# A hybrid decoder trunk on one core: where five short serial stretches stand, and what is moved around them

## The reference, cut to what matters

```
Layer i (i even: native sparse attention, i odd: gated DeltaNet):
  h = RMSNorm(x); proj = h @ W_in[i] -> [token-mixer columns | memory-query columns]
  token mixer (causal) in parallel with 4-head cross-attention into 256 memory tokens
  x = x + concat(mixer_out, memory_out) @ W_out[i]
  x = x + relu(RMSNorm(x) @ W_up[i])**2 @ W_down[i]
y = RMSNorm(x)
```

## Time and profile before

| | us |
|---|---|
| median of 3 runs | 1996.64 (1996.47 to 1998.94) |
| the profiled execution | 2001.48 |
| its span, first to last instruction | 1999.7 |
| PE busy in it | 1893.6 (95%) |
| DVE busy | 1049.5 |
| ACT busy | 520.3 |

### The profile page before, as it was taken

The page is one execution under the profiler, slowest core; times in us unless marked ns, Lnnn a source line. Parts: engine busy times, 40 slices in busy tenths (PEclk is TensorE's granted clock), DMA queues, the critical chain, the costliest instruction groups (busy, mean ns, idle before and its releaser), DMA issues.

```text
span 1999.7 us, 26775 instructions
## 1 busy us (share of the span) xinstructions
PE 1893.6 (95%) x10027; PEld 1522.5 (76%) x10027; DVE 1049.5 (52%) x2334; ACT 520.3 (26%) x1294; POOL 39.5 (2%) x48
## 2 busy tenths in 40 slices
PE   7999999998979999999989999899998999999997
PEld 6788555666758888888877787688876888888885
DVE  4441777655565444454446665456555544444444
ACT  2221777233312212100012523333341212210000
POOL 0000000000001000000010000000000000000001
PEclk9999999999989999999999999999998999999998
DMA  6532200566422222222233112100012122222211
GB/s 229 190 129 64 80 1 1 169 195 184 149 106 84 85 85 84 73 78 83 85 121 136 64 64 68 74 1 1 32 41 72 66 85 85 84 85 85 85 64 45
DMA packets 60801, 175.46 MB, mean 88 GB/s; under 512 B 6529, under 2 KB 39442, under 8 KB 47362
## 3 DMA queue, kind: packets, MB, share of 16 engines
q1 hardware_dynamic: 58050, 163.05, 24.4%
q0 software_dynamic: 2624, 10.70, 1.3%
HBM read 160.80 MB, written 12.93 MB: 87 GB/s over the span
## 4 chain that ended last, share of the span: by engine, by line
PE 82%; DVE 6%; SPq 5%; ACT 4%; issue 3%; DMA 1%; POOL 0%; DVEq 0%; POOLq 0%; ACTq 0%
PE psum L1818 58%; PE psum L1341 5%; SPq L492 3%; PE psum L758 2%; PE psum L902 2%; SPq L487 1%; PE psum L739 1%; ACT sbuf L802 1%; PE psum L721 1%; DVE sbuf L1677 1%; PE psum L1796 1%; PE psum L641 1%; PE psum L1899 1%; PE psum L1893 1%; PE psum L1931 1%
## 5 line engine op out<-in xcount | busy, mean ns | idle before, releaser
L1818 PE MATMUL psum<-sbuf 128*128 128x272 f32 x5152 | 1196.1, 393 | 4.5 <-ACT sbuf L2093 1.4
L1818 PEld LDWEIGHTS psum<-sbuf 128*128 128x128 f32 x5152 | 972.7, 190 | 215.6 <-issue 11.3
L1341 PE MATMUL psum<-sbuf 128*128 128x128 f32 (+3 forms) x1020 | 125.8, 279 | 12.4 <-DVE sbuf L1661 5.2
L1341 PEld LDWEIGHTS psum<-sbuf 128*128 128x128 f32 (+3 forms) x1020 | 118.7, 191 | 19.5 <-DVE sbuf L1661 6.0
L2043 ACT ACTIVATE sbuf<-sbuf 128x544 f32<-128x544 f32 x32 | 20.8, 651 | 396.9 <-DVE sbuf L2387 387.5
L902 PE MATMUL psum<-sbuf 128*128 128x256 f32 x448 | 106.7, 389 | 7.1 <-DMA sbuf<-in_pages 7.1
L2266 DVE TENSOR_TENSOR sbuf<-sbuf 128x512 f32<-128x512 f32 x92 | 63.4, 689 | 81.4 <-PE psum L1818 73.6
L902 PEld LDWEIGHTS psum<-sbuf 128*128 128x128 f32 x448 | 82.8, 190 | 24.0 <-DMA sbuf<-in_pages 8.1
L2270 DVE TENSOR_TENSOR sbuf<-sbuf 128x512 f32<-128x512 f32 x92 | 63.8, 693 | 52.2 <-PE psum L1818 50.5
L1520 ACT ACTIVATE sbuf<-psum 128x384 f32<-128x384 f32 (+2 forms) x84 | 40.2, 480 | 106.0 <-PE psum L1341 80.8
L2279 DVE TENSOR_TENSOR sbuf<-sbuf 128x512 f32<-128x512 f32 x92 | 63.1, 686 | 0.0
(11 more groups left out here) (390 smaller groups left out, 2026.9 us busy)
## 6 DMA issues: line engine op xcount, KB each, us to landing
sbuf<-in_w SPq DMA_DIRECT2D x100, 1024.0 KB, 4.9
sbuf<-in_pages SPq DMA_DIRECT2D x256, 128.0 KB, 2.4
sbuf<-in_mcache SPq DMA_DIRECT2D x2, 4096.0 KB, 15.4
sbuf<-in_win SPq DMA_DIRECT2D x8, 512.0 KB, 4.8
out_win_o<-sbuf POOLq DMA_DIRECT2D x8, 512.0 KB, 3.0
sbuf<-in_state SPq DMA_DIRECT2D x6, 512.0 KB, 5.7
out_state_s<-sbuf POOLq DMA_DIRECT2D x6, 512.0 KB, 3.1
sbuf<-in_x SPq DMA_DIRECT2D x1, 2176.0 KB, 11.9
```

Source lines behind the costliest of these rows:

```text
L1341: last = mm(bank(pair[x])[0:rows, width * (h - h0):width * (h - h0 + 1)], lhs(h), rhs(h), start=True, stop=True)
L1818: ins = mm(to, lhs(k), rhs(k), start=first and k == 0, stop=k == 3, skip_group_check=True)
```

## The change

1. **Begin.** SP issues panel 1 before x. PE does three products into an unused bank as soon as the constants are there (`idle_work`), then sums each of the memory tokens' squares as it comes. The squares of x are added on DVE into `rstd` (seven additions, `first_squares`, behind the 16 `memn`), and PE makes only two products for them (`first_norm_sums`), which stand between the memory keys and values of layer 0 and those of layer 1. The first half of layer 0's keys waits for `memn` tile by tile.
2. **Norms 2 and 4.** PE sums the squares with the tokens as output partitions: ten matmuls of one column, five from `sq_sum` and five from the last tile (`token_norm_sums`). DVE adds the two (128x5), ACT takes the root and DVE the reciprocal of 128x5, and PE spreads the result over the partitions with six matmuls against the identity, into banks 6 and 7. `norm` reads it there. `single` of the second input layer therefore goes into banks 4 and 5.
3. **Entry of the recurrence.** The gates of chunk 0 are made in unit 11 of the input layer, with the two memsets, the running sums on PE behind the first product of unit 12 (in banks 4 and 5), the exponents on DVE in unit 12, the exponentials and the root on ACT between its last two reads of unit 12. Behind the last product PE starts at once with k·k and q·k of chunk 0, and waits for the last read only after them. The SiLU of the last gates is waited for in the last chunk.
4. **Exit of the recurrence.** The reciprocal of the samples' lengths and the weight sums stand ahead of the last state addition on DVE; `spread_samples` stands behind the first product of the output layer, and its scaling on DVE behind the memory part of the input sums (`after_last`).

```diff
@@ begin
             panel(0)
+            panel(1)
             sp.dma_start(xT, x_in).then_inc(in_x, 16)
-            for i in range(1, 4):
-                panel(i)
+            panel(2)
+            panel(3)
...
             def memory_sums():
                 pe.wait_ge(in_common, 16)
-                pe.wait_ge(mem_sq, KT)
+                idle_work(pe, 5, 3)
                 for k in range(KT):
+                    pe.wait_ge(mem_sq, k + 1)
                     last = mm(bank(0)[:, 0:MEM], ones, sqm[:, k, :], start=k == 0, stop=k == KT - 1)
...
             memory_sums()
-            for k in range(KT):
-                square_sums(k)
-            memory_kv()
+            memory_kv(0)
+            first_norm_sums()
+            memory_kv(1)
...
+            def first_squares():
+                for k in range(1, KT):
+                    dve.wait_ge(sq_ready, k + 1)
+                    if k > 1:
+                        dve.wait_ge(dve_step, k - 1)
+                    tt(rstd, rstd, sq[:, k % 2, :], ALU.add).then_inc(dve_step, 1)
@@ norms 2 and 4
+            def token_norm_sums(n):
+                pe.wait_ge(sq_added, 6 * n)
+                for ci, at in enumerate(BLOCKS):
+                    mm(bank(6)[:, ci:ci + 1], sq_sum[:, at:at + P], ones[:, 0:1], start=True, stop=True)
+                pe.wait_ge(sq_ready, (n + 1) * KT)
+                for ci, at in enumerate(BLOCKS):
+                    last = mm(bank(7)[:, ci:ci + 1], sq[:, 1, at:at + P], ones[:, 0:1], start=True, stop=True)
+                last.then_inc(sq_used, 1)
+                pe.wait_ge(dve_step, RSTD_READY[n])
+                for ci, lo, hi in SPREADS:
+                    half, at = lo // HALF, BLOCKS[ci]
+                    last = mm(both(3)[:, half, lo - HALF * half:hi - HALF * half],
+                              rstd_t[:, ci:ci + 1].to_broadcast([P, P]), ident[:, lo - at:hi - at], start=True, stop=True)
+                last.then_inc(pe_step, 1)
@@ entry
+                    if (g, place) == (GDN_U - 1, 1):
+                        running_sums(pe, 0)
...
+                if not ci:
+                    pe.wait_ge(*read_out(ubase["gdn_in"] + GDN_U - 1, "c11"))
+                    pe.wait_ge(dexp_ready, 1)
...
+                    if t == 2 * GDN_U - 2:
+                        decays(act, 0)
+                        act.wait_ge(ks_read, 1)
+                        f(kr, kr2, ACT.Sqrt).then_inc(kr_ready, 1)
...
+                    if g == 11:
+                        decay_rows(dve, 0)
+                        dve.memset(st_p, 0.0)
+                        dve.memset(wq, 0.0)
+                    if g == 12:
+                        exponents(dve, 0)
@@ exit
+            def samples_between(g, place):
+                if (g, place) == (0, 1):
+                    spread_samples(pe)
+                if (g, place) == (0, 2):
+                    pe.wait_ge(cn_ready, GH + 1)
...
+                        dve.wait_ge(cn_std, 2)
+                        dve.reciprocal(rinv[0:TS, 4, :], rinv[0:TS, 4, :]).then_inc(cn_rec, 1)
+                        before_last()
                     dve.wait_ge(sdec_ready, h + 1)
                     dve.wait_ge(snew_mm, h + 1)
                     tt(sg[h], sg[h], view(banks(6, 2), 2, 4, P), ALU.add).then_inc(snew_ready, 1)
-            before_last()
-            dve.wait_ge(cn_std, 2)
-            dve.reciprocal(rinv[0:TS, 4, :], rinv[0:TS, 4, :]).then_inc(cn_rec, 1)
+            after_last()
             dve.wait_ge(cn_bc, GH + 1)
```

More of the change, by code:

```diff
@@ L615, in build, with idle_work @@
         scored = lambda g: 8 * (g // 2) + 1 + max(m for m in range(8) if PAIR[m][0] == g % 2)
+        def idle_work(pe, b, n):
+            for _ in range(n):
+                pe.matmul(bank(b)[:, 0:256], ident, common_ap[:, 0:256], start=True, stop=True)
         def compress_prompt(pe):
@@ L1328, in spread_samples, with decay_rows, running_sums, exponents @@
             last.then_inc(cn_bc, 1)
+        sums_in = lambda ci: BD if ci else (4, 5)
+        def decay_rows(dve, ci):
+            R, U = CHUNKS[ci][0], GC["cum" if ci < 4 else "cum_s"]
+            dve.tensor_tensor(ug[0:R, :, 0:R], U[0:R, 0:R].unsqueeze(1).to_broadcast([R, GH, R]),
+                              bcast(gat[0:R, ci, :], R, GH, R), ALU.mult).then_inc(ug_ready, 1)
+        def running_sums(pe, ci):
+            R = CHUNKS[ci][0]
+            pe.wait_ge(ug_ready, ci + 1)
+            pe.wait_ge(nwt_ready, 2 * ci)
+            for x, (h0, h1) in enumerate(HALVES):
+                last = pe.matmul(bank(sums_in(ci)[x])[:, 0:R * (h1 - h0)], ones[0:R, :], ug[0:R, h0:h1, 0:R],
+                                 start=True, stop=True)
+            last.then_inc(gc_done, 1)
+        def exponents(dve, ci):
+            R, MASK = CHUNKS[ci][0], GC["mask" if ci < 4 else "mask_s"]
+            dve.wait_ge(gc_done, ci + 1)
+            for x, (h0, h1) in enumerate(HALVES):
+                for h in range(h0, h1):
+                    last = dve.scalar_tensor_tensor(
+                        out=dec[0:R, h, 0:R], in0=bank(sums_in(ci)[x])[0:R, R * (h - h0):R * (h - h0 + 1)],
+                        scalar=gcn[0:R, ci, h:h + 1], in1=MASK[0:R, 0:R], op0=ALU.subtract, op1=ALU.subtract)
+            last.then_inc(gc_ready, 1)
+        def decays(act, ci):
+            R = CHUNKS[ci][0]
+            act.wait_ge(gc_ready, ci + 1)
+            act.activation(dec[0:R, :, 0:R], dec[0:R, :, 0:R], ACT.Exp, scale=-1.0)
+            for x, (h0, h1) in enumerate(HALVES):
+                last = act.activation(egr[:, h0:h1, 0:R], view(bank(sums_in(ci)[x])[:, 0:R * (h1 - h0)], h1 - h0, R),
+                                      ACT.Exp)
+            last.then_inc(dexp_ready, 1)
         def pe_gdn(pe):
@@ new lines, in memory_kv @@
+            def memory_kv(l):
+                pe.wait_ge(in_panel[2 * l], 16)
+                wk, wv = view(ring[2 * l], KT, MEM), view(ring[2 * l + 1], KT, MEM)
+                for hp in range(2):
+                    for k in range(KT):
+                        if hp == 0:
+                            pe.wait_ge(memn_ready, KT * l + k + 1)
+                        last = mm(bank(1 + 2 * l)[:, MEM * hp:MEM * (hp + 1)], wk[:, k, P * hp:P * (hp + 1)],
+                                  memn[:, l, k, :], start=k == 0, stop=k == KT - 1)
+                last.then_inc(pe_out, 1)
+                pe.wait_ge(in_panel[2 * l + 1], 16)
+                for m in range(2):
+                    for k in range(KT):
+                        last = mm(bank(2 + 2 * l)[:, MEM * m:MEM * (m + 1)], memn[:, l, k, P * m:P * (m + 1)],
+                                  wv[:, k, :], start=k == 0, stop=k == KT - 1)
+                last.then_inc(pe_out, 1)
```

161 lines of the change are left out of this document (65 added, 96 removed).

## The result

The changed kernel takes 1984.90 us, the median of five executions from 1978.18 to 1985.44, against 1996.64, which is a median of five too. The ratio is 0.9933 with a 95% interval from 0.9922 to 0.9943: faster by 0.7%, where 1.3% was forecast, and 5 us above the range's upper end. The profiled execution took 1984.69 (span 1982.9). Against the 2001.48 of the profiled execution before, that is 16.8 us, where the sum promised 26.8; between the medians it is 11.7.

The account below looks back on a forecast made before the run. PE, busy for 95% of the span, was taken as the bound. Gains of 9.1 + 3.2 + 1.3 + 8.7 + 4.5 = 26.8 us off the median of 1996.64 gave 1970, range 1966 to 1980.

Parts of the forecast that it names:

- the sum: Whole kernel: gains at begin, norm 2, norm 4, entry and exit add up to 26.8 us.
- The clock eats a part: PE's new gaps and the exit leave it at 1.2 GHz: gain 19.2 us, time 1977, chance 0.20.
- the fall of the clock in the idle 2.8 us: Begin, ahead of layer 0's keys: the clock might fall while PE idles, costing another 1.7 us.
- PE's idle spell falls apart into two of about 1 us, so the clock should stay up: Norm 2: the product behind was to take 7.37 us and not 9.13, another 1.8 of the 3.2 us gain.
- the size of the spreading: Norm 2: 12 records on PE at 0.145 us each, 1.75 us in all.
- the bound that was given: Norm 4: gain of 0.3 us with spreading at the lower clock, where 1.3 was forecast.
- the decays don't hide: Entry, unit 12: ACT's exponentials come late and PE waits ahead of k·k; gain 21.1 us, time 1975.5, chance 0.09.
- slower: Recurrence: the clock falls before its first chunk and stays down, +57 us at full length; chance 0.04.
- I take 4.5, a clock that rises between: Exit: gain of 4.5 us, taken between 2.2 at the lower level and 6.3 at best.
- the upper bound of 6.3: Exit: the first output product brings the clock up at about 1512, DVE becomes the limit, gain 6.3 us at best.
- the 0.5 us that the prediction estimated: Norm 4: reading the scale from PSUM makes the eight scalings 0.5 us longer; not added to the sum.

Follow-up runs that it names:

- the kernel with all fills: Changed kernel plus idle products ahead of layer 0's keys, and wide sums with two idle products in norms 2 and 4 and at the exit: 1969.36 us, ratio 0.9856.

## Why the prediction came out as it did

**The direction was right, and the mechanism was one of its rivals.** "The clock eats a part" gave 19.2 us and a chance of 0.20. The trace gave 16.8, and each of its places is the one that the rival named; the time of 1977 it missed too, for a reason given below. And the kernel with all fills, which adds to PE's work and differs in the clock, gives 1969.4. That the parts are worth less is out: with all fills the kernel is 1998.18 - 1969.36 = 28.8 us ahead of the one before, more than the 26.8 of the sum; the exit alone then gives 6.8 and not 4.5. A reading of the prediction was off as well: PE's second longest wait, 7.9 us at L974 for DVE's L1176, is missing from its list of the largest; the change leaves it as it is.

**Begin.** The step that failed is the value taken between its bounds: the fall of the clock in the idle 2.8 us stood there as a bound (1.7) and was left out of the sum. It happened (1.9) in all seven profiles that have this gap behind the change's own idle products: the keys took 8.85 us in six and 8.74 in one. It did not come in the gap, but 1.3 us into the keys, and in the kernel without the change's idle products the same gap went without it (7.17). The memory's sums ended 0.5 late, inside their range. Removing x's squares, the additions that hide behind the keys and the scalings that end before `single` all went as worked out.

**Norm 2.** The step that failed reads "PE's idle spell falls apart into two of about 1 us, so the clock should stay up". It argued from the length of the gap alone and took no account of the work ahead of it: behind the one-column records the clock fell in all seven profiles, in one of them with the gap of 1.00 us filled; behind 96-column records of nearly the same duration, in front of the same gap, it stayed up, in the one profile that has the width without a filling and in two that have both. With that fell the size of the spreading (1.75 forecast, 2.77 measured; 1.52 where the clock stayed up) and of the product. The -1.1 of the table is not the price of the change: it sets 17.50 against an execution whose old norm 2, at 16.38, was the quickest of three. On average the gain is 0.6. That the rival had 0.6 too is chance: by the terms beside it, 1.4 less the 1.25 that a spreading of 3 and not 1.75 costs and nothing from the product, it should have read 0.2.

**Norm 4** is the same step, with 0.3 at the lower level, the bound that was given.

**Entry.** Right in place and in size: 8.7 forecast, 9.0 between the traces, 8.6 by the kernel with the old entry, and 9.7 between the medians. The rival "the decays don't hide" is out: ACT was free at 1265.0 and waited 1.69 us for PE at its last read, where 1.6 were forecast. So is "slower": from 1267 to 1445 us, over the chunks of the prompt, the granted clock was 1.00. (Where the samples' chunk begins it was 0.83 for 20 us, in both kernels.) The table load that was moved costs what the earlier trace rows showed, 1.28 us, and the trace has the next operation 1.30 us behind its start. The Trainium skill (ScalarE: Activation LUTs, What ACT_TABLE_LOAD costs) gives 1283 ns for the load, with which the trace agrees, and a drain of 1380 ns besides, which this trace doesn't show; an estimate from that figure, 2.8 us for ACT's two loads in unit 12, would have eaten the 1.6 us that were left.

**Exit.** The step that failed is "I take 4.5, a clock that rises between". Its lower end was 2.2 for a clock that stays low until the end, and 1.9 was measured. The prediction read the lower level as coming "after idling", of 4.00 us, and let the first product, put directly behind the state products, bring the clock up at about 1512. But the kernel before was at that level ahead of those 4.00 us: its granted clock was 0.95 in the window at 1504 us and 0.50 at 1505, and its last state products already took 3.77 us, against 1.98 in the heads before. Its timeline, 1491 to 1545 us:

```profile
1505.12 0.80 PE L1311 MATMUL psum<-sbuf 128*32 128x1 f32 x12 [0.82 <-ACT sbuf L1501]
1505.85 3.77 PE L1468 MATMUL psum<-sbuf 32*128 32x512 f32 x4
```

The changed kernel keeps this piece as it is, and the clock falls there again, at 1490 us. It was back 17 us later in both profiles, with the 4.00 us idle or busy, and 7 us later in the three of the changed exit that took 18.0. So closing the gap did not by itself bring the clock back sooner. Over seven profiles the changed exit lies at 21.54, 18.0 (three times), 21.53, 21.55 and 20.05, on average 19.8, against 22.7 for the two of the kernel before: 2.9. With the fill it is 15.9, 6.8 less, a little above the upper bound of 6.3, and then DVE's reads are the limit (waits of 0.41, 1.05 and 0.62 us in PE's timeline), as that bound had it.

**The sum's base.** The profiled execution before, 2001.48, lay 4.8 above its median, and two of the stretches with a price here differ by 1.4 us between its executions. A further 3.3 us between two executions of the kernel before lie in the 989 us from `single` to norm 2, which the change doesn't touch; what makes them I haven't found. This is also why the medians are further off than the traces: 11.7 and not 26.8 is 15.1 short, 10.0 by the parts and 5.1 because the profiled execution before was slow for its kernel and the one after was not. Measured again, the changed kernel was 19.5 ahead (1998.18 - 1978.69), inside the prediction's range and close to the rival's 19.2. Which of the two medians one gets is luck, so the number says less about the rival than its four places do.

**PSUM as a source.** The eight scalings took 5.62 us with the scale in PSUM, against 5.66 from SBUF. The sum added nothing for it and was right; the 0.5 us that the prediction estimated from the Trainium skill (VectorE: DVE Perf Modes, TRN2 errata) are not there.

**Open.** What decides whether the clock falls in a single execution: the same instructions gave norm 2 in 15.95 and 17.50, and the exit in 18.0 and 21.54 us. Nor is it settled whether wide sums alone would do in every execution, at norm 2 or at norm 4: one profile shows them. The four executions with all fills scatter by 2.6 us, the eleven of the changed kernel by 14, so much of the scatter comes from these stretches. Not all of it does: the part between `single` and norm 2 took from 983.9 to 989.0 us in twelve of the thirteen profiles and 994.5 in the other, with the same instructions.

## What to carry to other kernels

Where a change shortens an idle spell of TensorE, price the work behind the gap at both clock levels, look at what stands ahead of the gap as well as at its length, and take the lower level unless a row shows otherwise. Work that is hidden before the bottleneck needs it, like the entry's, gives its full price; work that only leaves a smaller gap may give nothing until the clock is held there. A stretch that ends with narrow products and a wait is worth wider products and a few idle ones in the wait, which here together, with the begin's gap filled too, turned 0.9% into 1.4%. Filling alone did not do at norm 2, nor width alone at the exit.

## What the runs showed of the hardware

- Records of one column keep PE busy in the profile (2.4 us for twenty, share 1.00 in the window that they fill), yet in all seven profiled executions with one-column sums at norm 2 work behind them ran at the level of 1.2 GHz (9.0 to 10.6 us for the 32 records); in the three profiled with 96 columns, two of them with the gap filled as well, it ran at 2.4 GHz (7.61). The wider sums lasted 0.1 us longer. At the exit 64 columns without a filling made no difference (3.78 us for the state products). The Trainium skill (TensorE: Matmul & The Clock Gate, Part 1) says that the gate follows how busy TensorE has been recently. PE's busy share in the profile doesn't tell the two kernels apart, and no run here shows what the gate takes for busy.
- Idle time ahead of a product doesn't say at which level it runs: 2.96 us gave 8.85 in one kernel and 7.17 in another, and none at all (with idle products behind one-column sums) still gave 2.77 for the spreading.
- The same program's time scatters by 14 us in 1980 over eleven executions where such stretches are left to chance, and by 2.6 over four where they are filled. With the stretches filled and the old entry, four executions lie within 1.1 us and a fifth 10.4 above them.
